# Hybrid decoder layer on one core: attention steps that hold several token blocks, and output weights split during the last merge

## Reference

```python
h = rmsnorm(x, norm_g)
proj = h @ w_in
...
logits = logits + (cb[..., :, None] - c[..., None, :])        # A: forgetting attention, 8 heads
...
_, sel = lax.top_k(score, top_k)                              # B: the 256 best keys of an indexer, 8 heads
...
merged = (jax.nn.sigmoid(ga) * (ya @ w_a) + jax.nn.sigmoid(gb) * (yb @ w_b)
          + jax.nn.sigmoid(gc) * (yc @ w_c))
return (x + merged @ w_o).astype(x.dtype)
```

## Time and profile before

| | |
|---|---|
| median of 3 runs | 1528.29 us (1521.99 to 1529.33) |
| the profiled execution, own time | 1528.18 us |
| its span, first to last instruction | 1526.2 us |
| TensorE busy | 1440.7 us, 94% |
| TensorE weight load busy | 1132.0 us, 74% |
| VectorE busy | 727.6 us, 48% |
| ScalarE busy | 695.9 us, 46% |
| mean granted TensorE clock | 0.982 |

### The profile page before, as it was taken

The page is one execution under the profiler, slowest core; times in us unless marked ns, Lnnn a source line. Parts: engine busy times, 40 slices in busy tenths (PEclk is TensorE's granted clock), DMA queues, the critical chain, the costliest instruction groups (busy, mean ns, idle before and its releaser), DMA issues.

```text
span 1526.2 us, 20911 instructions
## 1 busy us (share of the span) xinstructions
PE 1440.7 (94%) x7890; PEld 1132.0 (74%) x7890; DVE 727.6 (48%) x1568; ACT 695.9 (46%) x1482; POOL 64.8 (4%) x133
## 2 busy tenths in 40 slices
PE   4978899999999999999999999999999999999898
PEld 3756667777776778887777777777777778888686
DVE  5363865545565894555434334543333346232524
ACT  6253666656675452111555565454544433211412
POOL 1102210000000000000000000100000000000000
PEclk9987999999999999999999999999999999999999
DMA  5115511111111112222111000312222221222422
GB/s 169 26 30 136 132 50 34 35 35 29 35 35 36 35 42 62 76 76 76 43 29 28 22 22 15 117 49 52 88 70 73 87 84 42 69 83 83 145 83 97
DMA packets 112131, 96.58 MB, mean 63 GB/s; under 512 B 10528, under 2 KB 97952, under 8 KB 111776
## 3 DMA queue, kind: packets, MB, share of 16 engines
q1 hardware_dynamic: 100816, 58.54, 14.4%
q0 software_dynamic: 11216, 36.71, 7.7%
HBM read 72.95 MB, written 18.09 MB: 60 GB/s over the span
## 4 chain that ended last, share of the span: by engine, by line
PE 86%; DVE 6%; ACT 4%; issue 2%; DMA 1%; SPq 1%; DVEq 0%; ACTq 0%; POOL 0%; POOLq 0%
PE bank L750 21%; PE bank L752 21%; PE bank L751 20%; PE bank L928 6%; PE bank L909 6%; PE slot L900 4%; PE slot L885 2%; DVE idle_out L1336 1%; PE slot L750 1%; PE slot L752 1%; PE slot L751 1%; ACT pta L1189 1%; DVE score L1477 1%; ACT relu_t L1122 1%; ACT ptb L1189 1%
## 5 line engine op out<-in xcount | busy, mean ns | idle before, releaser
L750 PE MATMUL bank<-hs,w_hl 128*128 128x512 f32 x1152 | 463.9, 403 | 9.6 <-DVE tm L1582 5.5
L752 PE MATMUL bank<-hs,w_hl 128*128 128x512 f32 x1152 | 452.6, 393 | 0.0
L751 PE MATMUL bank<-hs,w_hl 128*128 128x512 f32 x1152 | 452.0, 392 | 0.0
L1309 DVE TENSOR_TENSOR w_hl<-w_raw,w_hl 128x512 fp32r<-128x512 f32 (+1 forms) x176 | 118.9, 679 | 355.9 <-ACT w_hl L1019 353.8
L750 PEld LDWEIGHTS bank<-hs,w_hl 128*128 128x128 f32 x1152 | 218.7, 190 | 55.8 <-issue 9.9
L752 PEld LDWEIGHTS bank<-hs,w_hl 128*128 128x128 f32 x1152 | 218.0, 189 | 47.6
L751 PEld LDWEIGHTS bank<-hs,w_hl 128*128 128x128 f32 x1152 | 218.7, 190 | 43.8 <-issue 0.8
L1019 ACT ACTIVATE w_hl<-w_raw 128x512 fp32r<-128x512 f32 (+1 forms) x176 | 109.1, 622 | 196.5 <-PE bank L752 186.6
L1336 DVE TENSOR_SCALAR_CACHE_REDUCE idle_out<-score,state 128x768 uint8<-128x768 f32 (+3 forms) x140 | 115.3, 824 | 4.8
L1207 ACT ACTIVATE idle_out<-score,state 128x896 bf16<-128x896 f32 x64 | 70.3, 1098 | 17.1 <-DVE state L1332 16.0
L1495 DVE CUSTOM_DVE_ANT_0 slot<-slot,score 128x128 f32<-128x128 f32 (+7 forms) x64 | 47.3, 781 | 46.1 <-PE slot L900 46.1
(11 more groups left out here) (297 smaller groups left out, 2115.8 us busy)
## 6 DMA issues: line engine op xcount, KB each, us to landing
w_raw<-in_w_in_dram SPq DMA_DIRECT2D x142, 256.0 KB, 2.8
merged_scratch<-ms POOLq DMA_DIRECT2D x16, 512.0 KB, 3.5
ms<-merged_scratch POOLq DMA_DIRECT2D x16, 512.0 KB, 4.1
xn<-in_x_dram SPq DMA_DIRECT2D x8, 512.0 KB, 6.6
iq_st<-iq_hl POOLq DMA_DIRECT2D x32, 128.0 KB, 2.6
qb<-qb_scratch POOLq DMA_DIRECT2D x8, 512.0 KB, 4.7
w_raw<-in_w_o_dram SPq DMA_DIRECT2D x16, 256.0 KB, 3.7
qb_scratch<-bq_high POOLq DMA_DIRECT2D x4, 512.0 KB, 3.0
```

Source lines behind the costliest of these rows:

```text
L750: pe.matmul(out_, wh, mh, start=start, stop=False)
L751: pe.matmul(out_, wh, ml, start=False, stop=False)
L752: return pe.matmul(out_, wl, mh, start=False, stop=stop)
L1309: v.tensor_tensor(lo, src, hi.bitcast(F32), ALU.subtract).then_inc(w_low, 1)
```

## The change

- Branch c: a unit holds two neighbouring token blocks in the first two dilation groups (four units per channel) and four in the third (two per channel). Each block is a segment with its own columns in the slot; it has its own bias pass and exponential, and one value bank and one copy serve the unit.
- Branches a and b: blocks 0 and 3 form one unit and 1 and 2 another, the second segment at column 512, so both use two slots; blocks 4 to 7 stay alone. Six units per channel.
- A pick follows every unit in channels 0 to 3 of c and two follow every unit in channels 4 and 5.
- Filler per step: 3 pieces in c (6 in channel 4), 2 in a (but for its last channel), 2.2 in b; before 1.6, 1.6 and 1.68.
- Last merge: gates 6 and 7 come ahead of product 5 (the last gate in a buffer of its own), one chunk is split behind each of the last six pieces, and the weight splits may run past the merge's last block, so output blocks 0 and 1 are split there; the layout of the output weights puts these in memory that is free by then.

```diff
-RATE_B = 0.84
+RATE_B = 2.2
...
+WIDE_UNITS = (((3, 0), (0, HALF)), ((2, 0), (1, HALF)), ((4, 0),), ((5, 0),), ((6, 0),), ((7, 0),))
...
-    def pair_run(units, before, rate):
+    def units_of(br, ch):
+
+        if br != "c":
+            sets = [[dict(b=b, at=at, W=P * (b + 1)) for b, at in unit] for unit in WIDE_UNITS]
+        elif ch // 2 == 2:
+            sets = [[dict(b=b, at=P * (b % 4), W=P) for b in range(b0, b0 + 4)] for b0 in (0, 4)]
+        else:
+            sets = [[dict(b=b, at=2 * P * (b % 2), W=P * min(b + 1, 2) if ch < 2 else P * (b % 2 + 1))
+                     for b in (b0, b0 + 1)] for b0 in range(0, TB, 2)]
+        return [dict(br=br, ch=ch, b=min(x["b"] for x in segs), segs=segs) for segs in sets]
+
+    def pair_run(units, before):
...
-                x["slots"] = 2 if x["W"] > HALF else 1
-                x.update(S=nxt("S", x["slots"]), L=nxt("L", 2), unit=nxt("unit"))
+                x["slots"] = 2 if max(y["at"] + y["W"] for y in x["segs"]) > HALF else 1
+                x.update(S=nxt("S", x["slots"]), L=nxt("L", 2 * len(x["segs"])), unit=nxt("unit"))
...
-                parts = [(hh, c) for hh in range(2) for c in range(x["W"] // P)]
+                parts = [(hh, y["at"] // P + c) for hh in range(2) for y in x["segs"] for c in range(y["W"] // P)]
...
-                if units[s]["br"] == "c" and s % 2 == 1:
-                    pick()
+                if units[s]["br"] == "c":
+                    for _ in range(1 if units[s]["ch"] < 4 else 2):
+                        pick()
             x = units[min(s, n - 1)]
-            if x["br"] == "a" and x["ch"] == NCH["a"] - 1:
-                pump(1 if x["b"] >= 4 else 0)
+            if x["br"] == "a":
+                pump(2 if x["ch"] < NCH["a"] - 1 else 1 if x["b"] >= 4 else 0)
+            elif x["br"] == "c":
+                pump(6 if x["ch"] == NCH["c"] - 2 else 3)
             else:
-                pump(2 * rate)
+                pump(RATE_B)
...
-            if c + 1 < KC:
-                yield from tile_pieces("g" + br, c + 1, "h", br=br)
-            if br == "b" and c == KC - 2:
-                step("m_split", chunks=range(4))
-            yield from tile_pieces("w" + br, c, "y", chunks=n, br=br, gate=tiles["g" + br, c])
-            if br == "b" and c == KC - 2:
-                step("m_split", chunks=range(4, KC - 2))
+            ahead = {KC - 3: (KC - 2, KC - 1), KC - 2: (), KC - 1: ()} if br == "b" else {KC - 1: ()}
+            for g in ahead.get(c, (c + 1,)):
+                yield from tile_pieces("g" + br, g, "h", br=br)
+            for th, _ in enumerate(tile_pieces("w" + br, c, "y", chunks=n, br=br, gate=tiles["g" + br, c])):
+                if br == "b" and c >= KC - 3:
+                    step("m_split", chunk=2 * (c - KC + 3) + th)
+                yield
...
-        wo_hl = [at(64, "wo0", [P, 2, KC, HALF], F32R), at(16, "wo1", [P, 2, KC, HALF], F32R)]
+        wo_hl = [at(64, "wo0", [P, KC, 2, HALF], F32R), at(16, "wo1", [P, KC, 2, HALF], F32R)]
...
+        def wo_of(half, cc):
+            return wo_hl[half][:, (cc + KC // 2) % KC]
+
+        def gate_of(br, c, th):
+            if br == "b" and c == KC - 1:
+                return last_gate[:, th * HALF:(th + 1) * HALF]
+            return tm[:, 2 * (c % 2) + th, :]
...
+                    for i, seg in enumerate(a["segs"]):
+                        n = seg["W"] // P
+                        first = seg["b"] // 2 * 2 if a["br"] == "c" and a["ch"] // 2 == 1 else seg["b"] + 1 - n
+                        for c in range(n):
+                            for hh in range(2):
+                                t, j = at_part[hh, seg["at"] // P + c]
+                                cols = slice(HD * hh, HD * hh + HD)
+                                values = V["b"][:, c, :] if a["br"] == "b" else V[a["br"]][a["ch"] % 2][:, first + c, cols]
+                                ins = pe.matmul(bank[a["pv"][0]][cols, i * P:(i + 1) * P], values, PT[a["br"]][:, t, j, :],
+                                                start=c == 0, stop=c == n - 1)
...
-                        split_high(min(a["n"] + SPL, info["first_wo"]))
+                        split_high(min(a["n"] + SPL, info["first_wo"] + KC // 2))
...
+                        for j, seg in enumerate(a["segs"]):
+                            act.wait_ge(logit_ready, logit_of(a, j if a["slots"] == 2 else len(a["segs"]) - 1, hh) + 1)
+                            mx, dn = stats_of(a, j, hh)
+                            ins = A(PR[a["br"]][:, hh, seg["at"]:seg["at"] + seg["W"]], slot_of(a, seg, hh), ACTF.Exp, bias=mx,
+                                    scale=-1.0, accum_out=dn)
...
+                    br, ch, segs = a["br"], a["ch"], a["segs"]
                     full(act, a["pv"])
-                    y, src = Y[br][:, ch, :], bank[a["pv"][0]][:, 0:P]
-                    if br == "c" and ch // 2 == 2:
-                        y = y.rearrange("q (u c) -> q c u", c=16)[:, 2 * b:2 * b + 2, :]
-                        src = src.rearrange("q (c u) -> q c u", c=2)
+                    y, src = Y[br][:, ch, :], bank[a["pv"][0]][:, 0:P * len(segs)]
+                    if br == "c":
+                        b, n = a["b"], len(segs)
+                        if ch // 2 == 2:
+                            y = y.rearrange("q (u c) -> q c u", c=16)[:, 2 * b:2 * (b + n), :]
+                            src = src.rearrange("q (c u) -> q c u", c=2 * n)
+                        elif ch // 2 == 1:
+                            y = y.rearrange("q (x r) -> q r x", r=4)[:, b // 2, :]
+                        else:
+                            y = y[:, b * P:(b + n) * P]
+                        ins = A(y, src, ACTF.Copy)
                     else:
-                        y = v_tokens(br, ch, y, b)
-                    A(y, src, ACTF.Copy).then_inc(bank_free[a["pv"][0]], 1)
+                        for i, seg in enumerate(segs):
+                            ins = A(y[:, seg["b"] * P:(seg["b"] + 1) * P], src[:, i * P:(i + 1) * P], ACTF.Copy)
+                    ins.then_inc(bank_free[a["pv"][0]], 1)
...
                 elif kind == "m_split":
+                    cc = a["chunk"]
                     for u in tiles["gb", KC - 1]:
                         full(act, u)
-                    for cc in a["chunks"]:
-                        act.wait_ge(mixed, mix_base["b"] + 2 * cc + 2)
-                        A(hs[:, 0, cc, :], mT[:, cc, :], ACTF.Copy, scale=0.25).then_inc(m_high, 1)
+                    act.wait_ge(mixed, mix_base["b"] + 2 * cc + 2)
+                    A(hs[:, 0, cc, :], mT[:, cc, :], ACTF.Copy, scale=0.25).then_inc(m_high, 1)
                 elif kind == "final":
...
+                        for j, seg in enumerate(a["segs"]):
+                            o = slot_of(a, seg, hh)
+                            if a["br"] == "a":
+                                diagonal = o[:, seg["W"] - P:seg["W"]]
+                                then(v.tensor_tensor(diagonal, diagonal, tri_b[:], ALU.add))
+                            v.tensor_tensor_reduce(o, o, logit_bias(a, seg, hh), -slope, 0.0, ALU.add, ALU.min,
+                                                   stats_of(a, j, hh)[0]).then_inc(logit_ready, 1)
```

More of the change, by code:

```diff
@@ L234, in attend @@
                     before.setdefault(at - 5 + i if ch else 0, []).append(bcast)
-            for b in range(TB):
-                W = {0: P * min(b + 1, 2), 1: P * (b % 2 + 1), 2: P}[ch // 2] if br == "c" else P * (b + 1)
-                units.append(dict(br=br, ch=ch, b=b, W=W))
-        pair_run(units, before, 0.8)
+            units += units_of(br, ch)
+        pair_run(units, before)
         flush()
@@ L330, in build_plan @@
     pump(3)
-    pair_run([dict(br="b", ch=ch, b=b, W=(b + 1) * P) for ch in range(NCH["b"]) for b in range(TB)], {}, RATE_B)
+    pair_run([unit for ch in range(NCH["b"]) for unit in units_of("b", ch)], {})
     flush()
@@ L876, in _ @@
                         g, qt, kt = a["ch"] // 2, Q[br][a["ch"] % 2], K[br][a["ch"] % 2]
[L877 to L886 removed]
+                        for seg in a["segs"]:
+                            b, W = seg["b"], seg["W"]
+                            for hh in range(2):
+                                rows = slice(HD * hh, HD * hh + HD)
+                                if g == 0:
+                                    keys = kt[rows, (b + 1) * P - W:(b + 1) * P]
+                                elif g == 1:
+                                    keys = kt[rows, :].rearrange("q (x r) -> q r x", r=4)[:, b // 2, 0:W]
+                                else:
+                                    keys = v_tokens(br, a["ch"], kt[rows, :], b)
+                                ins = pe.matmul(slot_of(a, seg, hh), v_tokens(br, a["ch"], qt[rows, :], b), keys,
+                                                start=True, stop=True)
@@ L917, in _ @@
                     claim(pe, a["pv"])
-                    n = a["W"] // P
```

(17 more changed lines are left out.)

108 lines of the change are left out of this document (47 added, 61 removed).

## The result

The changed kernel takes 1529.03 us (median of 20 executions, 1525.52 to 1531.6); the kernel before, run beside it on the same chip, 1521.99 (1518.6 to 1529.33). The ratio is 1.0032, 95% interval 1.0019 to 1.0045: 4.9 us slower (2.9 to 6.8). The two medians lie 7.0 apart, but those of the kernel before are spread in two groups, 12 executions up to 1522.6 and 8 from 1524.3 on, so the ratio is the better measure. I forecast 1527, 0.8 faster. The time lies in the range and the difference is under 0.5%, but its sign is not the forecast one. That 1529 is so near 1527 is luck: my 1527 started from three executions of the kernel before with a median of 1528.3, and the median of twenty is 6 lower.

The account below looks back on a forecast made before the run. TensorE, busy 94% of the span, was taken to bound the kernel. From 1528.2 us, 25.6 gained and 24.8 lost made it 0.8 faster, 1527.4, say 1527; the 8-in-10 range was 1508 to 1539.

Parts of the forecast that it names:

- the price of a step (0.52): Dilated branch: each attention step costs TensorE a constant 0.52 us for changes between kinds of work, beyond the work itself.
- Gain 1: Dilated branch: 48 steps become 20, the matmuls stay, saving 28 x 0.52 = 14.6 us of TensorE's time.
- loss 2: Dilated branch, channels 2 to 5: wide strided copies free banks late, costing 3.2 us, bounds 0 and 5.
- the drain: End of the dilated branch: two steps drained without filler; three pieces left for each would gain 1.5 us.
- Loss 1: Dilated branch: picks ahead of bank reads on ScalarE and VectorE hold TensorE up, 21.6 us lost, bounds 4 and 27.
- Gain 2: Long branches: 64 steps become 48; joining saves 6.5 us, a third transpose group costs 5; net 1.6, bounds -3 and +3.
- Even: Forgetting branch, channel 3: longer exponential waits, about 1.6 and 2.7, offset by two waits of 0.3 and two steps gone.
- Gain 3: Last merge and output start: two TensorE waits and the half clock behind go, 7.9 us gained, bounds 4 and 8.
- rival 1: Dilated branch: picks hide, ScalarE and VectorE reach bank reads in time; 1510 us, or 1503 without small waits; chance 0.20.
- rival 2: Long branches: turns wait for value banks and third transpose groups, 13 us more, less 1.6 assumed: 1542; chance 0.15.
- rival 3: The end: early output splits block VectorE and the gaps move into the last merge; 7.9 us goes, 1535; chance 0.05.
- rival 4: TensorE: changes of kind cost nothing, by the skill's rule on weight loads pulled ahead; 1542 us; chance 0.03.

Follow-up runs that it names:

- The third kernel: The changed kernel with the dilated branch as in the kernel before (one block a step, a pick every second step); ratio 0.9968 to the kernel before, 4.9 us under.

## Why the prediction went wrong, point by point

- **What bounds the kernel, and the price of a step (0.52).** Right as a mechanism, for the dilated branch. A dilation-1 pair, 3.63 in single steps, takes 3.25 here (from 232.75, the last projection start, to the second one at 236.45, less two starts of 0.23), so the join gives back 0.38. The steps beside it take 3.02, but they have less work in them (1.81 and 1.60 in single steps): 0.39. A dilation-16 four takes 3.92, of which 0.75 is the stand at the second transposes (next point); the other 3.17 against 4.67 are 1.50 for three joins, 0.50 each. What in a change of kind costs this time no run here takes apart.

```profile
232.75 0.39 PE L781 MATMUL bank<-hs,w_hl 128*128 128x512 f32 x1
233.07 1.13 PE L916 MATMUL slot<-kc,qc 64*128 64x256 f32 x8
234.14 1.09 PE L958 MATMUL bank<-ptc,vc 128*64 128x128 f32 x16
235.16 1.21 PE L940 MATMUL bank<-ident,pc 128*128 128x128 f32 x8
236.13 0.48 PE L779 MATMUL bank<-hs,w_hl 128*128 128x512 f32 x1
236.45 0.39 PE L780 MATMUL bank<-hs,w_hl 128*128 128x512 f32 x1
```

- **Gain 1 and loss 2 (net 12.9 with the drain).** Measured 11.5 (284.5 to 273.0 without picks). Mis-sized by 1.4, or by 2.0 if the 0.6 that picks cost the narrow branch is left out. A join gives back 0.38 at dilation 1 where I had 0.52, eight times, and least at dilation 4, which I had not read: single steps of 1.72 and 2.18 became 3.66, a gain of 0.24 instead of 0.52 less 0.1, eight times too. The rows show a six-block turn in two groups with 0.14 between them (the last two rows belong to the wide copy, below):

```profile
328.66 1.75 PE L916 MATMUL slot<-kc,qc 64*128 64x128 f32 x8
330.34 0.88 PE L958 MATMUL bank<-ptc,vc 128*64 128x128 f32 x12
331.15 0.66 PE L940 MATMUL bank<-ident,pc 128*128 128x128 f32 x4
331.95 0.44 PE L940 MATMUL bank<-ident,pc 128*128 128x128 f32 x2
...
440.01 0.66 PE L940 MATMUL bank<-ident,pc 128*128 128x128 f32 x4
441.21 0.66 PE L940 MATMUL bank<-ident,pc 128*128 128x128 f32 x4 [0.55 <-ACT yc L1237]
```

  The strided wide copy cost about what I had, 0.8: in channel 5 the second four transposes start 1.20 behind the first, where four take 0.45, and the profile puts 0.55 of that down as a wait.
- **Loss 1 (21.6).** Measured 21.6, and nearly term by term (predicted, then found): the wait of channel 4, 5.3 and 5.4; that of channel 5, 5.2 and 5.4, each with half clock behind it; the transposed v 1.0 and 1.2; the first step of channel 4, 0.5 and 0.5; channels 0 to 3 together 4 and 4.1, which is how far the changed kernel is behind the one without picks at the first logits of channel 4; clock 5.6 and 4.5. One name was wrong: in channel 4 TensorE was released last by the low part of the weight split, which stands in the same two queues behind the same picks.
- **Gain 2 (1.6).** The step that failed most: measured 1.0 lost, 2.6 less. The sparse branch gained 1.4, the forgetting branch lost 2.3 to 2.4. The saving was there and larger than I had (1.05 in a middle channel of either branch, so some 8 in all, an estimate, for the 6.5). But of the 7.4 "at most" for the third group of transposes I took 5, on the reason that the value copies free the other bank; it costs the full price, 1.0 in a middle channel, some 8 in all (an estimate). And what joining adds at the transposes of v and the `rowsT` products, 0.5 in each of the first three channels of the forgetting branch, I had put at nothing. So these three channels lose 1.4. "Even" for channel 3 without filler was wrong too: it loses 0.9 more. There I set two waits of 1.6 and 2.7, less the two that go, against the 2.08 of the earlier trace rows; found are

```profile
927.45 1.15 PE L931 MATMUL slot<-ka,qa 64*128 64x384 f32 x12 [1.32 <-ACT pa L1211]
...
934.71 2.18 PE L931 MATMUL slot<-ka,qa 64*128 64x512 f32 x12 [2.51 <-ACT pa L1211]
```

  with 6.8 us at half clock behind them, where before there were 3.4. I had put a clock term behind the waits of the picks and none behind these, though before's own profile has such a stretch at 925.8. The third kernel has the same two waits with only 3.4, so that the longer stretch (1.7 us more) goes with the execution; the 1.0 leaves it out.
- **Gain 3 (7.9).** Right by stretches, 7.5: both waits and the half clock behind them are gone. By whole times 4.7 (2.3 to 7.0); that difference is left open.
- **The sum.** By stretches 11.5 - 21.6 - 1.0 + 7.5 = 3.6 slower, inside the interval of the measurement. I had 0.8 faster, 4.4 off: 2.6 in gain 2, 1.4 in gain 1, 0.4 in gain 3. Terms of 25 on either side left a rest smaller than the error of the small ones, and the rest's sign was not mine to give.
- **The rivals.** The picks did not hide (rival 1); the rule of the Trainium skill that the scalar and vector engines are strictly in order ("TensorE: Matmul & The Clock Gate", section "Architectural detail: the array is 16× 32×32, not 1× 128×128") is what the timeline above shows, with 5.37 and 5.42. The banks of the long branches (rival 2) cost nothing like 13: no step waits for a value bank, and the third group costs 0.5 a joined step, price and wait of 0.24 together. The end did what it says (rival 3). A change of kind does cost (rival 4): without picks widening gained 10.9.

## What to carry to other kernels

Widening a step saves the bound engine a part of a constant, 0.24 to 0.50 a join here, but it also gathers the filler and the background work of several steps in one place. In this kernel the background work that two in-order engines share did least harm behind the read that is due (274.7 against 280.7) and with no more than one unit of it in a step. Moving the picks, going from four blocks to two in channels 4 and 5 and leaving one branch at single blocks turned 0.3% slower into 1.2% faster than the kernel before (the new end, 0.3%, is in both), with the same matmuls; grouping the operands of dilation 4 made it 1.5%. And where a forecast is the small difference of large terms, price each kind of step from its own row: the kinds taken as "even", or at the price of another, moved the sum by 4.0 here, five times the difference forecast.

## What the runs showed of the hardware

- The granted clock gives the kernel a spread of its own. The code up to the dilated branch is the same in all kernels, and took 193.3 to 198.8 us; the one execution with a mean clock of 0.991 was 5 us shorter than the median of the same kernel.
- TensorE's clock fell to half behind waits of 5.4 us, and also around waits of 2.1 to 2.6 (at 925.8 in the kernel before), but not behind those of 0.5 to 0.8 in the dilated branch. Nor does it always fall at the longer ones: the same wait of 2.08 in the forgetting branch has 3.4 us at half clock beside it in seven traces and none in that with the mean clock of 0.991.
- A matmul whose operands are read at every fourth fp32 element is about half as fast: eight logits in 1.68, the same eight from neighbouring elements in 0.85, and the branch shorter by 6.6. ScalarE's grouped writes that replace it cost TensorE no wait. The Trainium skill, "SBUF — State Buffer", section "Door 1: The DMA port swizzle (why `[64,N]` ≈ `[32,N]`)", says that an access which goes to a new line of 16 bytes pays a penalty, and every fourth fp32 is one. With that the runs agree. The same place gives 4 fp32 as how far one can stride for free, and with that they do not.
